# A two-block float32 decoder on one NeuronCore: new order at the edges between stages, and three coarse score sets copied as rectangles by ScalarE

## The reference, cut to what matters

```python
# block 1, x is 256 tokens x 1024
h = rmsnorm(x, norm_mix_pre)
gq, gk, gv, gg1, gr, pu, mq, mk, mv, gates = split(h @ w_in)
ya = gla_mixer(gq, gk, gv, gg1, gr, ...) @ w_branch_a      # 4 heads, dk = 64
yb = pool_mixer(pu, ...) @ w_branch_b
yc = moba_mixer(mq, mk, mv) @ w_branch_c
mixed = sigmoid(gates[0]) * ya + sigmoid(gates[1]) * yb + sigmoid(gates[2]) * yc
x = x + rmsnorm(mixed @ w_out, norm_mix_post)
h = rmsnorm(x, norm_ffn_pre)
x = x + rmsnorm((silu(h @ w_gate) * (h @ w_up)) @ w_down, norm_ffn_post)
# block 2
h = rmsnorm(x, norm1_g)
...                                                        # one wide projection
y_hg = hgrn2_scan(...)                                     # 8 heads, dk = 128
y_ml = mlstm_scan(...)
y_mb = ssd_scan(...)
mixed = gates[0] * (y_hg @ w_br_hg) + gates[1] * (y_ml @ w_br_ml) + gates[2] * (y_mb @ w_br_mb)
x = x + mixed @ w_out
x = x + conv_gated_ffn(rmsnorm(x, norm2_g))
return rmsnorm(x, final_g)
```

## Time and profile before

| | |
|---|---|
| Median of 3 runs | 1246.29 us (1244.24 to 1246.87) |
| The profiled execution | 1246.99 us, its span 1245.2 us |
| PE busy | 1152.8 us, 93% of the span |
| PEld busy | 1075.6 us, 86% |
| DVE busy | 788.8 us, 63% |
| ACT busy | 600.7 us, 48% |
| DMA | 182.60 MB read from HBM, 147 GB/s over the span |

### The profile page before, as it was taken

One profiled execution on the slowest core, in us unless ns is written; L12 is line 12 of the kernel. 1 busy time (PEld: TensorE's weight loads), 2 busy tenths in 40 slices (PEclk: granted clock), 3 DMA queues, 4 the chain that ended last, 5 costly groups with the idle time before them and its releaser, 6 DMA issues. The chain is left out here.

```text
span 1245.2 us, 20485 instructions
## 1 busy us (share of the span) xinstructions
PE 1152.8 (93%) x8388; PEld 1075.6 (86%) x8388; DVE 788.8 (63%) x981; ACT 600.7 (48%) x770; POOL 0.2 (0%) x4
## 2 busy tenths in 40 slices
PE   3998999988999998998998899899999898999997
PEld 3988899977999997998888799798998787999996
DVE  4457566576655556558879644775556665777776
ACT  4462545436343435566443454456454535555553
POOL 0000000000000000000000000000000000000000
PEclk9999899998999999999998999899999899999999
DMA  6423334554555554253322223352444354555450
GB/s 248 169 103 136 105 135 143 173 182 137 184 192 179 192 179 169 99 194 114 102 102 93 78 102 136 122 206 80 147 158 147 110 206 135 183 186 197 173 201 34
DMA packets 26959, 184.69 MB, mean 148 GB/s; under 512 B 3064, under 2 KB 3592, under 8 KB 5128
## 3 DMA queue, kind: packets, MB, share of 16 engines
q1 hardware_dynamic: 26312, 181.81, 41.9%
q10 hardware_dynamic: 576, 1.85, 0.5%
HBM read 182.60 MB, written 1.05 MB: 147 GB/s over the span
## 5 line engine op out<-in xcount | busy, mean ns | idle before, releaser
L281 DVE TENSOR_TENSOR wlo<-raw,whi 128x2048 fp32r<-128x2048 f32 x170 | 389.4, 2292 | 242.8 <-ACT whi L274 239.6
L286 PE MATMUL pp<-XH,whi 128*128 128x256 f32 x1696 | 488.6, 288 | 16.1 <-DVE HF L904 9.3
L286 PE MATMUL pp<-XL,whi 128*128 128x256 f32 x1696 | 483.9, 285 | 0.0
L286 PE MATMUL pp<-XH,wlo 128*128 128x256 f32 x1696 | 483.8, 285 | 0.0
L274 ACT ACTIVATE whi<-raw 128x2048 fp32r<-128x2048 f32 x170 | 324.1, 1908 | 90.7 <-PE pp L286 46.4
L286 PEld LDWEIGHTS pp<-XH,whi 128*128 128x128 f32 x1696 | 329.4, 194 | 26.1 <-DVE HF L904 10.6
L286 PEld LDWEIGHTS pp<-XL,whi 128*128 128x128 f32 x1696 | 329.3, 194 | 0.8
L286 PEld LDWEIGHTS pp<-XH,wlo 128*128 128x128 f32 x1696 | 329.1, 194 | 0.0
L286 PE MATMUL pp<-Y,whi 128*128 128x256 f32 x480 | 87.0, 283 | 0.0
L1490 ACT ACTIVATE Y<-P 128x256 fp32r<-128x256 f32 x44 | 18.4, 418 | 131.7 <-DVE P L1523 131.7
L286 PEld LDWEIGHTS pp<-Y,whi 128*128 128x128 f32 x480 | 75.3, 192 | 0.0
(11 more groups left out here) (289 smaller groups left out, 1408.4 us busy)
## 6 DMA issues: line engine op xcount, KB each, us to landing
raw<-stream SPq DMA_DIRECT2D x170, 1024.0 KB, 4.9
P<-gains ACTq DMA_DIRECT2D x3, 512.0 KB, 3.5
X<-xt SPq DMA_DIRECT2D x2, 512.0 KB, 4.7
out<-P SPq DMA_DIRECT2D x4, 256.0 KB, 2.3
C<-consts SPq DMA_DIRECT2D x1, 761.5 KB, 12.6
P<-rows_w ACTq DMA_DIRECT2D x1, 272.0 KB, 2.7
U<-poolw SPq DMA_DIRECT2D x1, 256.0 KB, 11.5
PC<-cols SPq DMA_DIRECT2D x1, 177.0 KB, 5.4
```

The lines of the kernel that those rows point to most:

```text
L281: dve.tensor_tensor(wlo[:, slot, :], raw[:, slot, :], whi[:, slot, :].bitcast(F32), ALU.subtract).then_inc(lo_ready, 1)
L286: done = pe.matmul(dst, a, b, start=first and n == 0, stop=last and n == 2, **kw)
```

## The change

1. **Start.** Each half of `x` has its own semaphore. ACT loads the square root's table ahead of everything, splits pair 0 between the norm and `turn_act` and pair 1 behind it, and goes on with the splits of pairs 2 to 4 ahead of the copy of `g1`. DVE makes `wlo` of pair 0 ahead of `XL`, writes `XL` directly (`turn_lo`), makes `wlo` of pair 1, and only then the float32 copy `HF` (`keep_dve`, semaphore `h_kept`). PE does the `G1W` matmuls behind pair 1, not behind pair 0.
2. **Start of block 2.** The same on DVE; the split of its pair 1 (pair 70 of the stream, BLK2 + 1) moves from the end of FFN 1 behind the turn. PE does the row matmuls (now L1055 and on) behind pair 0 as before, with a wait for `h_kept`.
3. **Mix edges.** `XH` and `XL` of tiles 0 to 3 are written between the last pairs of the window (`mix_act`, `lo_part`), and tiles 4 to 7 at its end. `load_sqrt` stands right behind them on ACT.
4. **Norm edges behind `w_out`.** The last split of the window stands behind the turn and not ahead of the norm. `load_sqrt` inside the norm is left for FFN outputs only (`use in (1, 3)`).
5. **Scores.** ACT takes sets 1, 2 and 3 by plain copies of the rectangles that are not zero; DVE keeps sets 0 and 4 to 8. PE computes set 2 for its 64 x 64 rectangles only.

```diff
@@ norm_act
-            if i == 0:
+            if i == 0 and use in (1, 3):
                 load_sqrt(act)
@@ pre_dve is now scale_dve, turn_lo and keep_dve
+    def keep_dve(dve, gain):
+        for j in range(KT):
+            i = dve.tensor_scalar(HF[:, j, :], turned(j), col(gain, j), None, ALU.mult)
+        i.then_inc(S("h_kept"), 1)
@@ gated_pe
+                    if n == 2:
+                        at = u * 128
+                        i = pe.matmul(pm[0:64, at_h + at + 64:at_h + at + 128], z[rows, tile, at:at + 64],
+                                      z[rows, tile, at + 64:at + 128], start=True, stop=True)
+                        continue
...
@@ gated_act
+        def copy_scores(n):
+            act.wait_ge(S("scores_ready"), 9 * r + n + 1)
+            taken_scores(act, r, 0)
+            ps = pm[:, 1024 * (n % 2):1024 * (n % 2) + 1024].rearrange("p (h u t) -> p h u t", h=4, u=2)
+            if n == 1:
+                i = act.activation(A[:, :, 1, :], ps[:, :, 0, :], ACT.Copy)
+            elif n == 2:
+                i = act.activation(A[0:64, :, 0::2, 64:128], ps[0:64, :, :, 64:128], ACT.Copy)
+            else:
+                for at in (0, 64):
+                    i = act.activation(A[at:at + 32, :, 0::2, at + 32:at + 64], ps[at:at + 32, :, :, at + 32:at + 64], ACT.Copy)
+            i.then_inc(S("scores_copied"), 1)
...
         for n in range(8):
             if n or r < 2:
                 exponentials(n)
+            if n in COPIED:
+                copy_scores(n)
             st.go(1 if n % 2 == 0 or r == 0 and n < 5 else 0)
@@ ffn_side
-            turn_fn(eng, b, f + n, at % RING, at // RING if at < NPAIRS else None,
+            turn_fn(eng, b, f + n, at % RING, at // RING if at < NPAIRS and n < 32 else None,
@@ PE
         st.window(*W_START, 0)
-        st.go(1)
+        st.go(2)
         pe.wait_ge(S("tables_loaded"), 16)
+        pe.wait_ge(S("h_kept"), 1)
...
         st.window(*W_ROWS, 3)
         st.go(1)
+        pe.wait_ge(S("h_kept"), 2)
         pe.wait_ge(S("masks_rounded"), 3)
         rows_pe(pe, st)
@@ ACT, start
+        load_sqrt(act)
         norm_act(act, 0, loaded=True)
+        split_hi(act, 0, 0, 0)
         act.wait_ge(S("cols_loaded"), 16)
         turn_act(act, 0, 0, "norm_mix_pre")
-        st.start()
+        split_hi(act, 1, 1, 0)
+        st.window(*W_START)
+        st.go(3)
         act.wait_ge(S("g1_ready"), 1)
@@ ACT, mix of block 1 and the norm behind it
-        st.finish()
-        mix_act(act, 1)
+        st.go(3)
+        mix_act(act, 1, 0)
+        st.go(1)
+        mix_act(act, 1, 2)
+        st.go(2)
+        mix_act(act, 1, 4)
+        mix_act(act, 1, 6)
+        load_sqrt(act)
         act.dma_start(words(ROWS_W, 0, KT * 68), rows_w).then_inc(S("rows_w_loaded"), 16)
         act.dma_start(words(POST_GAIN[1], 0, D), gains[0]).then_inc(S("gain_loaded"), 16)
         st.window(*W_OUT)
-        st.finish()
+        st.go(3)
         norm_act(act, 1, use=0)
         norm_act(act, 2, updated=0)
         turn_act(act, 2, 1, "norm_ffn_pre")
+        st.finish()
...
         norm_act(act, 4, updated=4)
         turn_act(act, 4, 2, "norm1_g")
+        split_hi(act, BLK2 + 1, (BLK2 + 1) % RING, (BLK2 + 1) // RING)
@@ DVE, start
-        dve.wait_ge(S("x_loaded"), 32)
-        pre_dve(dve, 0, 0, "norm_mix_pre", True)
-        st.start()
+        scale_dve(dve, 0)
+        split_lo(dve, 0, 0)
+        turn_lo(dve, 0, "norm_mix_pre")
+        split_lo(dve, 1, 1)
+        keep_dve(dve, "norm_mix_pre")
@@ DVE, start of block 2
-        pre_dve(dve, 4, 2, "norm1_g", True)
+        scale_dve(dve, 4)
+        turn_lo(dve, 4, "norm1_g")
+        split_lo(dve, BLK2 + 1, (BLK2 + 1) % RING)
+        keep_dve(dve, "norm1_g")
```

More of the change, by code:

```diff
@@ L615, in add_dve, with scale_dve @@
             dve.tensor_tensor(chunk(h, c), chunk(h, c), acc(h, c), ALU.add).then_inc(S("x_updated"), 1)
-    def pre_dve(dve, n, r, gain, keep=False):
+    def scale_dve(dve, n):
         for h in range(2):
@@ L671, in lo_part, with mix_act @@
                                  ALU.mult, ALU.subtract).then_inc(S("x_lo"), 1)
-    def lo_parts(dve, base, scale=1.0):
-        for k in range(0, KT, 2):
-            lo_part(dve, base, k, scale)
-    def mix_act(act, b):
-        for k in range(0, KT, 2):
-            act.wait_ge(S(f"mixed_ready{b}"), k + 2 if b == 1 else k // 2 + 1)
-            act.activation(XH[:, k:k + 2, :], HF[:, k:k + 2, :], ACT.Copy, scale=0.5).then_inc(S("x_hi"), 1)
+    def mix_act(act, b, k):
+        act.wait_ge(S(f"mixed_ready{b}"), k + 2 if b == 1 else k // 2 + 1)
+        act.activation(XH[:, k:k + 2, :], HF[:, k:k + 2, :], ACT.Copy, scale=0.5).then_inc(S("x_hi"), 1)
     eps1, eps4, one, eps16 = (SC[:, 127:128], SC[:, 126:127], SC[:, 125:126], SC[:, 124:125])
@@ L741, in gated_pe @@
                 pe.wait_ge(S("gated_z_ready"), 2 * (8 * r + n))
-            if n >= 2 or r:
-                pe.wait_ge(S("scores_taken"), 9 * r + n - 1 if n >= 2 else 9 * r)
+            if n >= 2:
+                taken_scores(pe, r, n - 2)
+            elif r:
+                taken_scores(pe, r - 1, 8)
             if n == 1 and r:
@@ L764, in gated_pe @@
             i.then_inc(S("scores_ready"), 1)
-        pe.wait_ge(S("scores_taken"), 9 * r + 9)
+        taken_scores(pe, r, 8)
+        taken_scores(pe, r, 3)
         for h in range(4):
@@ L909, in gated_dve @@
                 y_low(1)
-            take(n)
+            if n in MASKED:
+                take(n)
             st.go(1 if n % 2 == 0 or r == 0 and n < 5 else 0)
@@ L1687, in _ @@
         st.window(*W_BRANCH2)
+        st.go(3)
+        mix_act(act, 2, 0)
+        st.go(1)
+        mix_act(act, 2, 2)
         st.finish()
-        mix_act(act, 2)
+        mix_act(act, 2, 4)
+        mix_act(act, 2, 6)
+        load_sqrt(act)
         st.window(*W_OUT2)
-        st.finish()
+        st.go(3)
         norm_act(act, 5, updated=8)
         turn_act(act, 5, 3, "norm2_g")
+        st.finish()
         act.dma_start(words(POST_GAIN[6], 0, D), gains[2]).then_inc(S("gain_loaded"), 16)
@@ L1707, in _ @@
         dve.wait_ge(S("cols_loaded"), 16)
-        dve.wait_ge(S("x_loaded"), 32)
-        pre_dve(dve, 0, 0, "norm_mix_pre", True)
-        st.start()
+        for h in range(2):
+            dve.wait_ge(S(f"x_loaded{h}"), 16)
+        scale_dve(dve, 0)
[3 more added lines that the diff above has]
+        keep_dve(dve, "norm_mix_pre")
         st.window(*W_START)
@@ L1724, in _ @@
         wait_evac(dve, W_BRANCH[0] - 1)
+        st.go(4)
+        lo_part(dve, 4 * mixes[1], 0, 0.5)
+        st.go(1)
+        lo_part(dve, 4 * mixes[1], 2, 0.5)
         st.finish()
-        lo_parts(dve, 4 * mixes[1], 0.5)
+        lo_part(dve, 4 * mixes[1], 4, 0.5)
+        lo_part(dve, 4 * mixes[1], 6, 0.5)
         st.window(*W_OUT)
+        st.go(3)
+        post_dve(dve, 1, 0)
+        scale_dve(dve, 2)
+        turn_lo(dve, 2, "norm_ffn_pre")
         st.finish()
-        post_dve(dve, 1, 0)
-        pre_dve(dve, 2, 1, "norm_ffn_pre")
         ffn_side(dve, 0, dve_turn)
         post_dve(dve, 3, 1)
-        pre_dve(dve, 4, 2, "norm1_g", True)
+        scale_dve(dve, 4)
+        turn_lo(dve, 4, "norm1_g")
+        split_lo(dve, BLK2 + 1, (BLK2 + 1) % RING)
+        keep_dve(dve, "norm1_g")
         st.p = BLK2
@@ L1756, in _ @@
         st.window(*W_BRANCH2)
+        st.go(3)
+        lo_part(dve, 4 * mixes[2], 0, 0.5)
+        st.go(1)
+        lo_part(dve, 4 * mixes[2], 2, 0.5)
         st.finish()
-        lo_parts(dve, 4 * mixes[2], 0.5)
+        lo_part(dve, 4 * mixes[2], 4, 0.5)
+        lo_part(dve, 4 * mixes[2], 6, 0.5)
         st.window(*W_OUT2)
+        st.go(3)
+        add_dve(dve, 2)
+        scale_dve(dve, 5)
+        turn_lo(dve, 5, "norm2_g")
         st.finish()
-        add_dve(dve, 2)
-        pre_dve(dve, 5, 3, "norm2_g")
         ffn_side(dve, 1, dve_turn)
```

35 lines of the change are left out of this document (18 added, 17 removed).

## The result

The changed kernel takes 1227.94 us (median of 4 runs, 1226.86 to 1228.98), the kernel before 1245.26 beside it (1239.32 to 1246.87): ratio 0.9856, 95% interval 0.982 to 0.9892, or 17.9 us less (13.4 to 22.4). In a second comparison of the same two it was 1229.51 against 1244.84, ratio 0.988 (0.9856 to 0.9904), 14.9 us less.

The account below looks back on a forecast made before the run. PE, busy 93% of the span, was taken to bound the kernel, so time saved where it waits is saved for good. Terms A to I summed to -11.7 us, giving 1235 us, range 1231 to 1240.

Parts of the forecast that it names:

- A: Start: PE's first product begins at 14.3 instead of 23.6 us, -9.3 us (-7 to -10.5).
- C: Mix of block 1: PE's 4.42 us wait goes, a new one of 2.1 comes, with 1.7 for the clock; -2.4 us.
- D: Norm behind the mix of block 1: ends sooner without the split and table load, -1.4 us (-1.0 to -1.8).
- H: Norm behind the mix of block 2: DVE's four additions shrink to one, table load goes; -1.6 us (-1.2 to -2).
- G: Mix of block 2: the wait of 2.20 us and 1.7 of half clock go, -3.9 us.
- E: Start of block 2: row matmuls wait for HF's last write, +2.6 us and 1.7 for the clock; +4.3 us.
- I: End: the table load comes at the last norm's first root with nothing to hide it, +1.3 us.
- made the start smaller: Rival at the start: loads or ACT's order hold the first pair, at most 4 us less gain, 1239; chance 0.10.
- the copies dear: Rival in the scores: ACT's copies of 32 and 64 partition slices are slower, 1250 at 3 us each; chance 0.03.
- The first rival: The clock doesn't fall in the two new waits, at the mix of block 1 and start of block 2: 1231.6; chance 0.18.
- B: Scores, r = 0: set 2's eight matmuls shrink to 64 columns on PE's path, -0.5 us (0 to -0.7).
- F: Scores, r = 1 and 2: ACT's copies stand ahead of exponentials in its queue, +1.8 us (0.9 to 3).

Follow-up runs that it names:

- e2: The changed kernel with the scores as before: DVE takes all nine sets, PE computes set 2 in full; 1229.65 us, ratio 0.9874.
- e3: The changed kernel with the eight writes of HF ahead of the low part of pair 70 at the start of block 2; 1226.20 us, ratio 0.9853.
- e5: The changed kernel with each rectangle copy on ACT behind the exponentials of the next set; 1227.97 us, ratio 0.9859.
- e6: The changed kernel with the early table load put back into the last norm, behind its first square; 1227.76 us, ratio 0.9857.
- e9: The changed kernel with the start of the kernel before; 1239.30 us, ratio 0.995 to the kernel before.
- e10: The kernel before with the change at the two mix edges and the norms behind them alone; 1237.57 us, ratio 0.9928.
- e4: The changed kernel with ACT's split of pair 34 ahead of the table load and DMA issues at the mix of block 1; 1227.89 us, ratio 0.9856.
- e11: The kernel before with the scores' part of the change alone; 1243.17 us, ratio 0.9986.
- e1: The kernel before with the new start alone; 1237.13 us, ratio 0.9934.
- the best kernel: The changed kernel with HF first, pair 34's split first, the last norm's early table load, and without the scores' part; 1219.35 us, ratio 0.9793.

## Why the prediction was wrong

**Right.** The waits: A -9.3 (measured -9.4), C's removed wait and its new one of 2.1 (2.09), D's and H's shorter norms (together with C's and G's waits -7.1 for -7.6), E's wait of 2.6 (2.67, and gone when `HF` is written first), I (1.28, and gone when the load moves). The rivals that made the start smaller and the copies dear didn't come: a copy of 64 x 512 takes 0.575 us and one of 32 x 256 0.374. That the waits sum to the forecast within 0.1 us is partly luck, as said below the table of both profiles. The drain of some 1.4 us that the Trainium skill (ScalarE: Activation LUTs, What ACT_TABLE_LOAD costs) adds to a switch of tables does not show here: in the row at 1216.99 above the root starts 1.30 us after the load began, and the end grew by 1.28.

**Wrong, the step that failed: the clock's account in C and E, 3 us of the 3.2 to 6.2 that the forecast lacks.** The prediction said "dense matmuls follow, so I take 1.7" in C and "by the same reading as in C the clock, 1.7" in E. That these short waits pull the clock down was read from two cases of the earlier trace rows. C's wait of 2.1 us stands in eight profiles (the change twice, e2, e3, e5, e6, e9, e10), with half clock behind it in one; E's of 2.5 to 3.1 in seven (the change twice, e2, e4, e5, e6, e9), also in one. So some 0.2 us each were due, not 1.7: 3 us of the miss. The first rival had this case, at 1231.6.

The two cases themselves were read rightly: the wait of 2.39 us ahead of the row matmuls (now L797) has half clock behind it in both scans of all 16 profiles, and the old wait of 2.20 us in three of the four profiles that have it (not in e11). What failed is to carry them over to other places by their length. Length alone doesn't decide: a wait of 2.10 us at L1296 (before L1260) had half clock behind it in 13 of 16. The matmuls around don't alone either: the old wait of 2.20 us and C's stand ahead of the same matmuls, L364. Longer waits are clear: of those of 4.2 us and more behind the start, 38 in all profiles together, each had it.

**Wrong, the untouched waits.** The prediction's sum gave the clock nothing at waits that the change leaves alone; only its range had 1.7 for them. Of the 6.2 us between the two profiles, 3.4 are the half clocks of the two old mix edges, which C and G had credited; the other 2.8 lie at places outside them, 1.7 of them at the end of the scan r = 2. How much of this an execution gets differs: by medians, the 17.9 and 14.9 us less the idle time of each profile (11.3 and 9.3) and the 2.2 of work leave 4.4 and 3.4 us for the clock, not 6.2, with intervals of +-4.5 and +-3 us. The mean granted clock tells the same, roughly, since it counts half clock in which PE waits too: 0.9725 over 67 executions of before, 0.9756 over 10 of the change; 0.0031 of 1235 us is 3.8.

**Mis-sized, B and F.** "The shorter set 2 lengthens a wait and gives nothing" counted only half: the waits of the scans grew by 3.3 us where F had 1.8 (r = 1 by 1.6 for 1.2, r = 2 by 1.6 for 0.6), while PE's work shrank by 2.2 in all three scans where B had 0.5. In sum +1.1 for a forecast of +1.3: two errors that cancel.

**Which part brings it.** In each row: microseconds by ratio, then what idle time and PE's score work of its profile explain.

| | by ratio | idle | score work | left |
|---|---|---|---|---|
| start alone (e1) | -8.2 | -9.4 | 0 | +1.2 |
| mix edges alone (e10) | -9.0 | -5.5 | 0 | -3.5 |
| scores alone (e11) | -1.7 | +2.7 | -2.1 | -2.3 |
| change without start (e9) | -6.2 | -1.7 | -2.2 | -2.3 |
| change, first comparison | -17.9 | -11.3 | -2.2 | -4.4 |
| change, second comparison | -14.9 | -9.3 | -2.2 | -3.4 |

The start brings nothing beside its waits that the profile of e1 shows; in the executions whose first matmuls are at full speed it saves another 1.3 to 2.6 us. The rest goes with the mix edges first, whose two old half clocks are gone in every version that has the new edges, and perhaps with the scores; with +-2 to 3 us in each row (+-4.5 for the first comparison) that is likely, not shown.

**Open.** What makes waits of 2 us differ by place, 1 in 8 at one and all of 32 at another; what decides between 3.4 and 6.8 us, or none, at a wait that two executions have alike; and why the best kernel has a mean clock of 0.980 with nearly the same waits as the one at 0.975.

## What to carry to other kernels

Add up waits and busy time apart: here the sum of the waits could be forecast within two microseconds from one trace, and the busy time moved by nearly as much with as many matmuls as before. The two new waits of 2 to 3 us cost their length, and half clock only twice in 15; those of 5 us at the same places cost the half clock as well. So removing a long wait is worth more than its length, and a short one in its place may cost little more than its length; but other waits of 2 us had half clock every time, so a short wait's clock is looked up in several profiles and not taken from its length. Write what is needed soon (`HF`) ahead of what is needed later (the next low part): the order of two DVE steps was worth 2.7 us of waiting, and a copy that stands ahead of another engine's input cost about as much as the shorter set 2 took off PE.
